# Turning the attention weights of a hybrid layer: 128x128 transposes on TensorE with a ScalarE copy, or 32x32 block transposes on VectorE

## The reference

```python
h = rms_norm_2(x, pre_w)
proj = h @ w_in                                  # 2048 -> 5952
y_a = diff_attention(...)                        # 4 heads, two softmaxes each, p0 - lam * p1
y_b = sliding_window_attention(qb, kb, vb, sinks)  # 16 heads of width 64, window 128
y_c = causal_attention(qc, kc, vc, ...)          # 4 heads
y = jnp.concatenate([y_a, y_b, y_c], axis=-1) * silu(gates)
out = y @ w_out
x = x + rms_norm_2(out, post_w)
```

## Time and profile before

| | us |
|---|---|
| median of three timed runs | 2535.49 |
| the profiled execution, its own time | 2531.34 |
| its span | 2529.5 |
| PE busy | 2484.5 (98%) |
| DVE busy | 1655.3 (65%) |
| ACT busy | 1130.8 (45%) |

### The profile page before, as it was taken

The page is one execution under the profiler, slowest core; times in us unless marked ns, Lnnn a source line. Parts: engine busy times, 40 slices in busy tenths (PEclk is TensorE's granted clock), DMA queues, the critical chain, the costliest instruction groups (busy, mean ns, idle before and its releaser), DMA issues.

```text
span 2529.5 us, 33166 instructions
## 1 busy us (share of the span) xinstructions
PE 2484.5 (98%) x13035; PEld 2048.8 (81%) x13035; DVE 1655.3 (65%) x2432; ACT 1130.8 (45%) x1942; POOL 0.2 (0%) x4
## 2 busy tenths in 40 slices
PE   5999999999999999999999999999999999999998
PEld 2678788888887888888888888888888888988887
DVE  2378689788945467666664566566567657656674
ACT  3422122223225545343453457456454746555563
POOL 0000000000000000000000000000000000000000
PEclk8999999999999999999999999999999999999999
DMA  9955466556634334534532344666534466644563
GB/s 371 364 178 172 138 191 213 184 177 206 249 134 145 101 96 157 171 99 163 165 108 83 93 141 165 218 217 186 183 134 167 167 233 195 191 160 141 167 217 133
DMA packets 356611, 440.88 MB, mean 174 GB/s; under 512 B 25390, under 2 KB 223848, under 8 KB 354536
## 3 DMA queue, kind: packets, MB, share of 16 engines
q1 hardware_dynamic: 348224, 414.25, 50.1%
q10 hardware_dynamic: 8232, 24.52, 2.6%
HBM read 430.29 MB, written 8.41 MB: 173 GB/s over the span
## 4 chain that ended last, share of the span: by engine, by line
PE 94%; ACT 2%; DMA 2%; DVE 1%; issue 0%; ACTq 0%; DVEq 0%; SPq 0%
PE ps L1342 16%; PE ps L1344 15%; PE ps L1343 15%; PE ps L1339 13%; PE ps L1340 13%; PE ps L1341 13%; DMA raw<-in_ada_w_dram 1%; PE ps L1363 1%; PE ps L2012 1%; PE ps L2020 1%; PE ps L1705 1%; PE ps L1734 1%; PE ps L1696 1%; PE ps L1709 1%; PE ps L1476 1%; PE ps L2038 0%
## 5 line engine op out<-in xcount | busy, mean ns | idle before, releaser
L2113 DVE TENSOR_TENSOR wl<-raw,wh 128x1024 fp32r<-128x1024 f32 (+2 forms) x614 | 695.4, 1152 | 391.2 <-ACT wh L697 387.1
L697 ACT ACTIVATE wh<-raw 128x1024 fp32r<-128x1024 f32 (+2 forms) x614 | 602.3, 1001 | 689.6 <-PE ps L1341 299.5
L1342 PE MATMUL ps<-wh,hTh 128*128 128x512 f32 (+1 forms) x1808 | 710.0, 393 | 3.8 <-DVE wl L2113 3.1
L1344 PE MATMUL ps<-wh,hTl 128*128 128x512 f32 (+1 forms) x1808 | 699.1, 387 | 0.0
L1343 PE MATMUL ps<-wl,hTh 128*128 128x512 f32 (+1 forms) x1808 | 698.2, 386 | 0.0
L1339 PE MATMUL ps<-hTh,wh 128*128 128x512 f32 (+1 forms) x1552 | 576.9, 372 | 0.9 <-ACT acc L969 0.7
L1340 PE MATMUL ps<-hTl,wh 128*128 128x512 f32 (+1 forms) x1552 | 573.1, 369 | 0.0
L1341 PE MATMUL ps<-hTh,wl 128*128 128x512 f32 (+1 forms) x1552 | 570.9, 368 | 0.0
L1342 PEld LDWEIGHTS ps<-wh,hTh 128*128 128x128 f32 x1808 | 339.9, 188 | 73.8 <-DVE wl L2113 4.2
L1344 PEld LDWEIGHTS ps<-wh,hTl 128*128 128x128 f32 x1808 | 339.7, 188 | 68.7
L1343 PEld LDWEIGHTS ps<-wl,hTh 128*128 128x128 f32 x1808 | 340.2, 188 | 63.7
(11 more groups left out here) (323 smaller groups left out, 1889.8 us busy)
## 6 DMA issues: line engine op xcount, KB each, us to landing
raw<-in_ada_w_dram SPq DMA_DIRECT2D x96, 1024.0 KB, 5.8
raw<-in_w_in_dram SPq DMA_DIRECT2D x88, 1024.0 KB, 5.1
raw<-in_ev_w_in_dram SPq DMA_DIRECT2D x192, 256.0 KB, 4.1
raw<-in_od_w_in_dram SPq DMA_DIRECT2D x384, 128.0 KB, 2.4
raw<-in_od_w_in_dram SPq DMA_DIRECT2D x32, 1024.0 KB, 5.0
raw<-in_w_out_dram SPq DMA_DIRECT2D x32, 1024.0 KB, 5.0
raw<-in_ev_w_out_dram SPq DMA_DIRECT2D x16, 1024.0 KB, 5.0
raw<-in_od_w_out_dram SPq DMA_DIRECT2D x16, 1024.0 KB, 5.0
```

The lines of the kernel that those rows point to most:

```text
L697: nc.scalar.activation(wh[:, ch.spl, part], raw[:, ch.raw, part], ACT.Copy).then_inc(s_hi, 1)
L1342: nc.tensor.matmul(out, x_h, w_h, start=first, stop=False, skip_group_check=True)
L1344: return nc.tensor.matmul(out, x_l, w_h, start=False, stop=last, skip_group_check=True)
L2113: nc.vector.tensor_tensor(wl[:, ch.spl, part], raw[:, ch.raw, part], wh[:, ch.spl, part].bitcast(F32), ALU.subtract).then_inc(s_lo, 1)
```

## The change

The six (or three) transposes on TensorE and the copy on ScalarE are gone. In their place VectorE turns the weights itself: 16 instructions for each pair, each of which reads one group of 32 partitions of `EX`, transposes all 32x32 blocks in it that belong to one 32-column position (6 blocks, or 3 for an "a" pair), and writes them to another group of 32 partitions. The result goes to two buffers in turn: even pairs to `PT` as before, odd pairs to the free end of `acc`. TensorE's weighing waits for VectorE's signal (`s_fl`) in place of ScalarE's. The flips leave `USE67`.

In VectorE's iteration the inversion of the sums keeps its place; the 16 transposes stand behind the low part of half i + 3.

```diff
-USE67 = [x for i in sorted(AFTER) for x in AFTER[i] if x.split()[0] in ("turn", "flip")]
+USE67 = [x for i in sorted(AFTER) for x in AFTER[i] if x.split()[0] == "turn"]
...
+        PTS = (PT, acc[:, 1, 0:6 * P].rearrange("p (m n) -> p m n", m=2))
...
-                def flip(n):
-                    act.wait_ge(s_fl, count(NPAIR, n + 1))
-                    if n:
-                        act.wait_ge(s_W, count(WEIGHED[NPAIR], WEIGHED[n]))
-                    k = 1 if PAIRS[n][0] == "a" else 2
-                    nc.scalar.activation(PT[:, 0:k, :], ps[:, 6:6 + k, 0:3 * P], ACT.Copy).then_inc(s_67, 1)
...
-                def flip(n):
-                    free67(f"flip {n}")
-                    pe.wait_ge(s_p, count(NPAIR, n + 1))
-                    for m in range(1 if PAIRS[n][0] == "a" else 2):
-                        for k in range(3):
-                            ins = nc.tensor.transpose(ps[:, 6 + m, k * P:(k + 1) * P], EX[:, m, k * P:(k + 1) * P], ident)
-                    ins.then_inc(s_fl, 1)
...
-                    pe.wait_ge(s_67, count(len(USE67), USE67.index(f"flip {n}") + 1))
+                    pe.wait_ge(s_fl, count(NPAIR, n + 1))
...
+                def turn_weights(n):
+
+                    blocks = lambda x: x.rearrange("p m (k n) -> p m k n", n=P)[:, 0:1 if PAIRS[n][0] == "a" else 2]
+                    dve.wait_ge(s_p, count(NPAIR, n + 1))
+                    if n > 1:
+                        dve.wait_ge(s_W, count(WEIGHED[NPAIR], WEIGHED[n - 1]))
+                    for i in range(4):
+                        for j in range(4):
+                            q, k = slice(32 * i, 32 * (i + 1)), slice(32 * j, 32 * (j + 1))
+                            ins = nc.vector.transpose(blocks(PTS[n % 2])[k, :, :, q], blocks(EX)[q, :, :, k])
+                    ins.then_inc(s_fl, 1)
...
                 for i in range(6, 2 * NPROJ - 1):
-                    flips(i)
+                    flips(i, flip)
                     if i + 3 < 2 * NPROJ:
                         split((i + 3) // 2, ((i + 3) % 2,))
+                    flips(i, turn_weights)
```

More of the change, by code:

```diff
@@ L1273, in after @@
                             turn_move(arg)
-                        elif verb != "weigh" or int(arg) == NPAIR - 1:
-                            {"score": score, "flip": flip, "weigh": weigh}[verb](int(arg))
+                        elif verb == "score":
+                            score(int(arg))
+                        elif verb == "weigh" and int(arg) == NPAIR - 1:
+                            weigh(int(arg))
                 def high_turned(n):
@@ L2037, in weigh @@
                                     out = ps[rows, 4 + m, 0:dv] if k < 2 else ps[rows, 4 + m, P:P + dv]
-                                    ins = nc.tensor.matmul(out, PT[:, m, k * P + c * 64:k * P + (c + 1) * 64], v[:, k % 2, w], start=(k != 1), stop=(k > 0),
+                                    ins = nc.tensor.matmul(out, PTS[n % 2][:, m, k * P + c * 64:k * P + (c + 1) * 64], v[:, k % 2, w], start=(k != 1), stop=(k > 0),
                                                            skip_group_check=True)
@@ L2043, in weigh @@
                         for k in range(2):
-                            nc.tensor.matmul(ps[:, 4 + m, 0:dv], PT[:, m, k * P:(k + 1) * P], v[:, k, w], start=(k == 0), stop=(k == 1), skip_group_check=True)
-                        ins = nc.tensor.matmul(ps[:, 4 + m, P:P + dv], PT[:, m, 2 * P:3 * P], v[:, 0, w], start=True, stop=True, skip_group_check=True)
+                            nc.tensor.matmul(ps[:, 4 + m, 0:dv], PTS[n % 2][:, m, k * P:(k + 1) * P], v[:, k, w], start=(k == 0), stop=(k == 1), skip_group_check=True)
+                        ins = nc.tensor.matmul(ps[:, 4 + m, P:P + dv], PTS[n % 2][:, m, 2 * P:3 * P], v[:, 0, w], start=True, stop=True, skip_group_check=True)
                     if kind != "b":
@@ L2083, in hyb_layer @@
                             turn_block(arg)
-                        elif verb != "move":
-                            {"score": score, "flip": flip, "weigh": weigh}[verb](int(arg))
+                        elif verb in ("score", "weigh"):
+                            {"score": score, "weigh": weigh}[verb](int(arg))
                     if i == 2 * NPROJ - 3:
@@ L3105, in after, with flips @@
                             weigh(int(arg))
-                def flips(i):
+                def flips(i, verb):
                     for what in AFTER.get(i + 1, []):
                         if what.startswith("flip"):
-                            flip(int(what.split()[1]))
+                            verb(int(what.split()[1]))
                 def low_turned(n):
```

## The result

The changed kernel takes 2650.7 us (median of four runs, 2648.5 to 2654.7) against 2533.8 us before (2531.5 to 2537.8): ratio 1.046, 95% interval 1.0446 to 1.0473. It is 117 us slower. The forecast was 2635 us, with a range of 2575 to 2695. The profiled execution took 2650.6 us, its span is 2648.8 us.

The account below looks back on a forecast made before the run. TensorE bounds the kernel before; with the change VectorE's loop with ScalarE does. Each layer gains 51.4 us in the stretch and about 1 in the tail, +104 us in both on 2531.34: 2635 us, range 2575 to 2695.

Parts of the forecast that it names:

- What is removed: TensorE's flips, 0.66 us for six transposes and 0.33 for three: 15.9 us in both layers at most; ScalarE's copies priced at nothing.
- T: Sixteen VectorE transposes of one pair, without overlap: 6.1 us, or 4.5 us for an "a" pair.
- Rival B: Transposes on VectorE overlap, 4.5 and 2.9 us for sixteen: 2590 us, about 2560 at bare element rate; chance 0.17.
- The closed loop: Score to score on VectorE and ScalarE, without TensorE: 11.1 us plus 6.1 makes a 17.2 us period, against TensorE's 13.0.
- Rival D: TensorE stays the bound and only its flips go, deciding at T = 1.9 us: 2515 us; chance 0.03.
- The stretch: First to last score of a hybrid layer: 242.3 us in place of 190.9, so +51.4 us.
- Pair 9 to 10: Span of eight halves with the rotation of k, ending in TensorE's turn, weighing, projections and score: 28.6 us.
- The clock: TensorE's clock in the score stretch: full clock expected; less would mean rival C.
- C: Loop as in the main forecast, but TensorE's clock falls in its new gaps: 2655 to 2700 us; chance 0.25.
- C's mild form: Clock falls in each gap, score takes 1.8 us not 0.9; 0.7 us on each of 28 periods: +20, 2655 us.
- VectorE's share: Sign in the new profile: VectorE busy near 85% of the score stretch, idle mostly in the 2.98 us ScalarE waits.
- The tail: Behind a layer's last score, another T and the last gate: TensorE ends about 1 us later still.

Follow-up runs that it names:

- run with one transpose: Changed kernel with one transpose over all 128 partitions in place of the sixteen, partition groups left as they are: 2520.9 us.
- run within the groups: Changed kernel with each of the sixteen transposes writing to the partition group that it reads: 2606.6 us.
- runs with T at 3.03, 4.64 and 6.11 us: Changed kernel with eight of the sixteen transposes (2571.2 us), with each transpose within its own partition group (2606.6 us), and as it is (2650.7 us).
- the reordering: Changed kernel with ScalarE's high part of the half behind a score ahead of the exponentials: 2613.1 us.
- the mixtures: Kernel before with ScalarE reordered and VectorE turning only some pairs, behind the weighing: pairs 0, 2, 4, 6, 8, 9 2551.3 us; without pair 9 2538.9 us.

## Why the prediction was right

- **What is removed**: 0.66 us for a flip, 16 us in all. The run with one transpose gained 13.0 us of it. With sixteen transposes the flips are worth nothing, as the run that keeps them shows.
- **T**: forecast 0.37 and 0.27 us for one, 0.38 and 0.28 from start to start, 6.1 and 4.5 us for sixteen. The rows have 0.369 and 0.270, and 6.11 and 4.51 for sixteen. The choice between overlap and none, made by the row of four instructions over 32 partitions, was the largest in the forecast (45 us), and it was right. Rival B falls for this order of groups; in the run within the groups, T is 4.64 us, close to B's 4.5. Both runs agree with the rule of the Trainium skill ("VectorE: DVE Perf Modes", "Two Vector instructions with no wait between them") that an instruction which starts in another group than the last one read or wrote waits for all earlier ones: 0.38 us start to start where the written group changes each time, 0.29 on average where it changes every fourth time.
- **The closed loop**: 17.15 us for a plain period, 17.2 forecast; the wait of 2.98 us unchanged. The runs with T at 3.03, 4.64 and 6.11 us have plain periods of 14.08, 15.68 and 17.15, each 11.04 or 11.05 us more than T; at 0.97 us TensorE's own 13 show. Rival D is the case of the one transpose. That it begins at T = 1.9 us is worked out from the two periods; the runs only put it between 0.97 and 3.03 us.
- **The stretch**: 242.3 forecast, 244.5 measured, in both layers. Pair 9 to 10: 28.6 and 28.87. The 2.2 us missing are four waits of 0.62 us in each layer for a score at half clock.
- **The clock** was not forecast right. The forecast had full clock in the stretches, "less means C", and the granted clock is 0.89 and 0.90. It fell in or right behind every one of TensorE's gaps of 2.38 us and more, 21 in the stretches and tails of both layers, so the condition of C's mild form was met nearly throughout. What was wrong there is C's price, 0.7 us in each of 28 periods: 12 scores ran at half clock, VectorE waited for 8 of them, since it was still busy at the others, and that is 5 us and not 20. The low clock mostly stretched TensorE's work into time in which it would have been idle: TensorE is busy for 203.6 us of the stretch, 83% and not the 75% forecast, where the run with one transpose needs 183.6 us for the same 1037 matmuls. VectorE's share is 80%, not 85%.
- **The tail** is the term that was mis-sized: "PE ends it about 1 us later still", and it is 5.6 and 6.7 us. TensorE's last weighing also needs banks 4 and 5, which VectorE frees with the weighing of pair 12, behind T of pair 13, the arithmetic of a gate and a low part. I had taken the hand-over of these banks into account for the scores and left it out here. The changed kernel shows 4.2 and 3.5 us of waiting there, and half clock behind it; the run with the last pair on TensorE removed the wait, and these two parts of its trace are 4.2 and 5.5 us shorter.
- The sum: 104 us forecast. 2 x 2.2 us of low clock and 2 x 5.2 us of tail are missing, which gives the 119 us of the spans. Both errors have the same sign, so the 2635 us are not the work of errors that cancel.

## What to carry to other kernels

A share of busy time doesn't tell how much an engine can take on: VectorE was idle a third of the time, and 40 us of new work in 65 us of idle time already made the kernel slower. Look for the loop that closes without the bounding engine, add up one round of it with the waits that belong to it, and compare with the bound's period: here 11.1 against 13.0 us, so 1.9 us were free in each pair, and not the 4.7 that 65 us over 14 pairs suggest. And where two engines run in fixed order, moving work or reordering one of them is priced by the same loop. But the sum over the loop alone promised too much there: the reordering gave two thirds of the forecast and the mixtures nothing, since other waits inside a round came up. The saved work of the old bound counts only until the new one takes over.

## What the runs showed of the hardware

- Sixteen VectorE transposes over 32 partitions with 192 float32 elements go start to start in 0.38 us if each writes to another group of 32 partitions than the one before, and in 0.29 us on average if it stays in its group for four in a row (T is 4.64 us in place of 6.11). One over 128 partitions with 768 elements takes 0.97 us: the same data in a sixth of the time, but without the move between groups.
- In the two stretches and tails of the changed kernel, between runs of dense matmuls of 10 us and more, TensorE's granted clock fell to 0.50 (its 1.2 GHz level) at every gap of 2.38 us and more. Behind the 14 gaps of 2.93 to 5.74 us it was at that level when TensorE started again. Behind the 7 gaps of 2.38 to 2.62 us the score still ran at 2.4 GHz, in 0.92 us, and the clock fell within 2 us of its start. Of the five gaps of 1.46 to 1.95 us, two were followed by a fall. The clock was back at its full level some 3 to 7 us after it fell.
- Most of these low spells cost nothing, since they stretched work into idle time: 20 us more of TensorE's busy time in a stretch, of which some 3 us for both layers reached the end of the first nine periods.
